# Gate and up weights in 4 MB transfers, and a scatter spread between the last tiles, in a hyena, mLSTM and mixture-of-experts block

## What is computed

```python
def ec_moe(h, w_router, w_gate, w_up, w_down):
    cap = CAP_FACTOR * L // N_EXPERTS                  # 64 tokens for each expert
    aff = jax.nn.softmax((h @ w_router).astype(jnp.float32), axis=-1)
    g, idx = lax.top_k(jnp.swapaxes(aff, 1, 2), cap)
    xs = jax.vmap(lambda hb, ib: hb[ib])(h, idx)
    a = jnp.einsum('becd,edf->becf', xs, w_gate)       # w_gate, w_up: 16 x 1024 x 2048
    u = jnp.einsum('becd,edf->becf', xs, w_up)
    ye = jnp.einsum('becf,efd->becd', jax.nn.silu(a) * u, w_down) * g[..., None]
    # ye's rows are added at their tokens' places; w_down: 16 x 2048 x 1024
```

## Time and profile before

| | |
|---|---|
| median of 3 runs | 1299.17 us (1297.36 to 1302.92) |
| profiled execution | 1296.7 us, its span 1294.7 us |
| TensorE matrix products busy | 1192.9 us, 92% |
| VectorE busy | 342.1 us, 26% |
| ScalarE busy | 164.3 us, 13% |
| GpSimd busy | 33.8 us, 3% |
| moved from memory | 453.02 MB, 352 GB/s over the span |
| DMA issues of gate, up, down tiles to the ring | 63, 63, 61 of 2048 KB, two of 1024 KB |

### The profile page before, as it was taken

One profiled execution on the slowest core, in us unless ns is written; L12 is line 12 of the kernel. 1 busy time (PEld: TensorE's weight loads), 2 busy tenths in 40 slices (PEclk: granted clock), 3 DMA queues, 4 the chain that ended last, 5 costly groups with the idle time before them and its releaser, 6 DMA issues.

```text
span 1294.7 us, 12923 instructions
## 1 busy us (share of the span) xinstructions
PE 1192.9 (92%) x5378; PEld 501.9 (39%) x5378; DVE 342.1 (26%) x625; ACT 164.3 (13%) x350; POOL 33.8 (3%) x61
## 2 busy tenths in 40 slices
PE   5899999999989999999979899998979898888997
PEld 2444454554444353353324253342324234232332
DVE  3775829346450020210201121010201110020140
ACT  2510020034420001000100010000101000000021
POOL 2000020000000001000000000000000000000000
PEclk9999999999999999999999999999999999999999
DMA  9966320306469999999999999999999999999997
GB/s 347 401 227 239 132 82 0 131 1 260 197 247 386 426 429 420 429 428 428 427 428 429 428 427 427 429 428 428 428 429 428 429 428 429 428 428 428 426 427 319
DMA packets 44867, 455.98 MB, mean 352 GB/s; under 512 B 6208, under 2 KB 6320, under 8 KB 16922
## 3 DMA queue, kind: packets, MB, share of 16 engines
q1 hardware_dynamic: 44098, 454.95, 84.2%
q0 software_dynamic: 464, 0.33, 0.1%
q10 hardware_dynamic: 264, 0.11, 0.1%
HBM read 453.02 MB, written 2.36 MB: 352 GB/s over the span
## 4 chain that ended last, share of the span: by engine, by line
PE 64%; DMA 29%; DVE 4%; ACT 1%; issue 1%; SPq 1%; POOL 0%; DVEq 0%; POOLq 0%
DMA ring<-in_w_exp_up 27%; PE B L1259 17%; PE B L1223 14%; PE B L775 6%; PE B L1166 4%; PE B L1022 4%; PE B L903 3%; PE B L1276 3%; PE B L968 2%; DMA ring<-in_pos 2%; PE B L825 2%; PE B L1240 1%; PE B L1176 1%; PE B L1003 1%; PE B L891 1%
## 5 line engine op out<-in xcount | busy, mean ns | idle before, releaser
L1223 PE MATMUL B<-ring,moe 128*64 128x512 f32 x2016 | 448.5, 595 | 64.5 <-DMA ring<-in_w_exp_up 34.8
L1223 PEld LDWEIGHTS B<-ring,moe 128*64 128x64 f32 x2016 | 139.5, 137 | 367.6 <-issue 250.3
L1259 PE MATMUL B<-ring,moe 128*64 128x512 f32 x992 | 217.0, 594 | 0.4 <-issue 0.3
L2219 DVE TENSOR_TENSOR moe<-moe,B 128x512 f32<-128x512 f32 x30 | 19.8, 684 | 611.5 <-PE B L1223 611.5
L1259 PEld LDWEIGHTS B<-ring,moe 128*64 128x64 f32 x992 | 69.8, 137 | 133.3 <-issue 131.1
L775 PE MATMUL B<-ring 128*128 128x512 f32 x192 | 83.6, 594 | 0.0
L1609 ACT ACTIVATE moe<-B 128x512 f32<-128x512 f32 x32 | 17.4, 594 | 385.2 <-PE B L1223 385.2
L1276 PE MATMUL B<-moe 128*128 128x512 f32 x128 | 63.1, 618 | 0.5
L1166 PE MATMUL B<-moe,xl 128*128 128x128 f32 x448 | 56.7, 287 | 1.9 <-DVE moe L2198 1.9
L1166 PEld LDWEIGHTS B<-moe,xl 128*128 128x128 f32 x448 | 55.5, 201 | 2.2 <-DVE moe L2198 2.2
L775 PEld LDWEIGHTS B<-ring 128*128 128x128 f32 x192 | 36.1, 190 | 45.1 <-issue 45.1
(11 more groups left out here) (383 smaller groups left out, 794.8 us busy)
## 6 DMA issues: line engine op xcount, KB each, us to landing
ring<-in_w_exp_up SPq DMA_DIRECT2D x63, 2048.0 KB, 30.0
ring<-in_w_exp_gate SPq DMA_DIRECT2D x63, 2048.0 KB, 28.4
ring<-in_w_exp_down SPq DMA_DIRECT2D x61, 2048.0 KB, 33.9
ring<-in_w_in SPq DMA_DIRECT2D x6, 2048.0 KB, 9.3
ring<-in_w_mod SPq DMA_DIRECT2D x10, 1024.0 KB, 7.5
ring<-in_w_mod SPq DMA_DIRECT2D x4, 2048.0 KB, 14.4
fr<-in_w_mod SPq DMA_DIRECT2D x6, 1024.0 KB, 9.4
ring<-in_w_out SPq DMA_DIRECT2D x2, 2048.0 KB, 7.8
```

Of the source, the lines that this page charges most:

```text
L1223: x = mm(B[2 * up + n // 2][rows, :], xst[:, 2 * q + k, CAP * e2:CAP * (e2 + 1)], w[:, k, n * CH:(n + 1) * CH], start=(q == 0 and k == 0), ...
L1259: x = mm(B[5][CAP * half:CAP * (half + 1), :], hdt[:, q // 2, k * P + at:k * P + at + CAP], wd[:, k, half * CH:(half + 1) * CH], start=(q ...
L2219: v.tensor_tensor(hid[:, m, :], sil[:, m, :], B[2 + m][:, :], ALU.mult).then_inc(S["v_hid"], 1)
```

## The change

Gate and up tiles take four rows to a partition: a block of 512 rows is two tiles, and partition p holds rows 4p to 4p + 3, of which the even tile has the first two and the odd one the last two. `pair_rows` becomes `quad_rows`, every fourth column of a 512-wide stretch, and the vectors, the router's weights and their copies follow. From group 1 on a new function, `expert_pair`, loads two tiles that are neighbours in the ring with one transfer of 4 MiB: for gate and up a piece is 32768 bytes, for down it stays 16384. SP waits for the second tile of a pair to be used and then issues both; TensorE waits only at the first tile of a pair. The tiles of a group go g, g, u, u, g, g, u, u, d, d, d, d, twice; the first expert keeps the old order (`FIRST_TILES`), and group 0 keeps single transfers, with the slots in another order (`SLOT_OF`) and the first loads ordered to suit. In the last expert, g0 g1, u0 u1 and g2 g3 come as pairs, and from tile 6 on (`SINGLE_FROM`) the tiles are single. In `gate_up` of the last expert each of the first four tiles is followed by two scatter products, each of the next three by two of the products that were L1377 (now `last_rows`); the last two and both turns stand behind the last up tile.

```diff
-def pair_rows(k):
-    return slice(2 * P * (k // 2) + k % 2, 2 * P * (k // 2 + 1), 2)
+def quad_rows(k):
+    return slice(4 * P * (k // 4) + k % 4, 4 * P * (k // 4 + 1), 4)
...
-        vr3 = slot(4, 3840, 4096)
+        vr3 = slot(7, 2048, 2560)
...
-        SLOT_OF = [3, 7, 6, 5, 0, 1, 4, 2]
+        SLOT_OF = [6, 7, 4, 5, 0, 1, 2, 3]
...
-            for q in range(4):
-                TILES += [("g", 4 * e2 + q), ("u", 4 * e2 + q)]
+            for q in (0, 2):
+                TILES += [(kind, 4 * e2 + q + n) for kind in "gu" for n in range(2)]
             TILES += [("d", 4 * e2 + q) for q in range(4)]
...
+        FIRST_TILES = [(kind, q) for q in range(4) for kind in "gu"] + TILES[8:]
+        SINGLE_FROM = 6
...
-                    src = w[0, bass.ds(ex, 1), q * 2 * P:(q + 1) * 2 * P, :]
-                    src = src.rearrange("o (p k) n -> p (o k) n", p=P)
+                    src = w[0, bass.ds(ex, 1), (q // 2) * 4 * P:(q // 2 + 1) * 4 * P, :]
+                    src = src.rearrange("o (p k) n -> p (o k) n", p=P)[:, 2 * (q % 2):2 * (q % 2) + 2, :]
...
+            def expert_pair(i, group, after=0):
+                kind, st = TILES[i]
+                e2, q = divmod(st, 4)
+                r = (ring_turn(i, False) - after * HALF) % NSLOT
+                at = SLOT_OF[r] * SLOTF
+                dst = ring[:, at:at + 2 * SLOTF]
+                ex = expert(group, e2, after)
+                if kind == "d":
+                    src = A["w_exp_down"][0, bass.ds(ex, 1), q * CH:(q + 2) * CH, :]
+                    src = src.rearrange("o (b p k) n -> p (o b) (k n)", b=2, p=P)
+                    dst = dst.rearrange("p (b n) -> p b n", b=2)
+                else:
+                    w = A["w_exp_gate" if kind == "g" else "w_exp_up"]
+                    src = w[0, bass.ds(ex, 1), (q // 2) * 4 * P:(q // 2 + 1) * 4 * P, :]
+                    src = src.rearrange("o (p k) n -> p (o k) n", p=P)
+                    dst = dst.rearrange("p (k n) -> p k n", k=4)
+                sp.dma_start(dst, src).then_inc(d_ring[r], 16)
...
             sp.wait_ge(S["p_w"], done_count("i", 5))
+            expert_tile(8, 0)
+            sp.wait_ge(S["p_num"], 16)
             expert_tile(0, 0)
-            sp.wait_ge(S["p_num"], 16)
-            expert_tile(2, 0)
             expert_tile(3, 0)
...
-            expert_tile(7, 0)
+            expert_tile(2, 0)
             sp.wait_ge(S["p_w"], len(DONE))
             expert_tile(4, 0)
             expert_tile(5, 0)
             sp.wait_ge(S["p_lg"], NLT)
             sp.wait_ge(S["p_g1"], 4)
-            expert_tile(8, 0)
+            expert_tile(7, 0)
             expert_tile(23, 0)
...
             with sp.Fori(1, ALONE - 1) as j:
-                for i in range(NTI):
-                    used(i, j)
-                    expert_tile((i + NSLOT) % NTI, j if i + NSLOT < NTI else j + 1)
+                for i in range(0, NTI, 2):
+                    used(i + 1, j)
+                    expert_pair((i + NSLOT) % NTI, j if i + NSLOT < NTI else j + 1)
...
-                    tr(B[0][:, 128:140], vr3[0:12, 0:2 * P:2], upper(12))
-                    tr(B[0][:, 140:152], vr3[0:12, 1:2 * P:2], upper(12)).then_inc(S["p_vt"], 1)
+                    for k in range(4):
+                        x = tr(B[0][:, 128 + 6 * k:134 + 6 * k], vr3[0:6, k:4 * P:4], upper(6))
+                    x.then_inc(S["p_vt"], 1)
...
-                pe.wait_ge(d_ring[r], NTI // NSLOT * 16 * group + 16 * (n + 1))
+                if first or r % 2 == 0:
+                    pe.wait_ge(d_ring[r], NTI // NSLOT * 16 * group + 16 * (n + 1))
...
+                for n, (kind, st) in enumerate(TILES[0:8]):
+                    if n == 0:
                         pe.wait_ge(S["v_xs"], 4 * group + 4)
+                    if n == (0 if last else 4):
                         pe.wait_ge(S["a_xs"], 4 * group + 4)
+                    products(kind, st)
+                    if last and n < NLT:
+                        scatter(group - 1, after, (2 * n, 2 * n + 1))
+                    elif last and n < 2 * NLT - 1:
+                        last_rows(n - NLT)
...
             gate_up(NGROUP - 1, 0, 1, False, True)
-            pe.wait_ge(S["v_yacc"], 8 * (NGROUP - 1))
-            for c in range(NLT):
-                if c == 2:
-                    turn(NGROUP - 1, 0, 1, 0)
-                for half in range(2):
-                    x = mm(B[5][CAP * half:CAP * (half + 1), :], peq[:, c, 0:CAP], y3[:, c, half * CH:(half + 1) * CH],
-                           start=(c == 0), stop=False)
-            x.then_inc(S["p_tail"], 1)
+            last_rows(NLT - 1).then_inc(S["p_tail"], 1)
+            turn(NGROUP - 1, 0, 1, 0)
             turn(NGROUP - 1, 0, 1, 1)
```

More of the change, by code:

```diff
@@ L438, in expert_tile @@
             def expert_tile(i, group, after=0, last=False):
-                kind, st = TILES[i]
+                first = isinstance(group, int) and group == 0
+                kind, st = (FIRST_TILES if first else TILES)[i]
                 e2, q = divmod(st, 4)
-                first = isinstance(group, int) and group == 0
                 r = (ring_turn(i, first) - after * HALF) % NSLOT
@@ L516, in _ @@
                     expert_tile(in_ring[n + NSLOT], 0)
-                else:
-                    expert_tile(n + NSLOT - len(in_ring), 1)
-            with sp.Fori(1, ALONE - 1) as j:
-                for i in range(NTI):
-                    used(i, j)
-                    expert_tile((i + NSLOT) % NTI, j if i + NSLOT < NTI else j + 1)
[L523 to L527, removed]
-                    expert_tile(HALF + i + NSLOT - NTI, ALONE, 1)
@@ new lines, in _ @@
+            for i in range(0, NTI, 2):
+                used(i + 1, ALONE - 1)
+                if i + NSLOT < NTI:
+                    expert_pair(i + NSLOT, ALONE - 1)
+                else:
+                    expert_pair(HALF + i + NSLOT - NTI, ALONE, 1)
+            for i in range(HALF, NTI, 2):
+                used(i + 1, ALONE, 1)
+                expert_pair((i + NSLOT) % NTI, ALONE if i + NSLOT < NTI else ALONE + 1, 1)
+            with sp.Fori(ALONE + 1, NGROUP - 2) as j:
+                for i in range(0, NTI, 2):
+                    used(i + 1, j, 1)
+                    expert_pair((i + NSLOT) % NTI, j if i + NSLOT < NTI else j + 1, 1)
@@ L536, in _ @@
+            for i in range(0, NTI, 2):
+                t = i + NSLOT - NTI
+                if t < SINGLE_FROM:
+                    used(i + 1, NGROUP - 2, 1)
+                    expert_pair((i + NSLOT) % NTI, NGROUP - 2 if t < 0 else NGROUP - 1, 1)
+                    continue
+                for n in range(2):
+                    used(i + n, NGROUP - 2, 1)
+                    expert_tile(t + n, NGROUP - 1, 1)
             for i in range(HALF - NSLOT):
@@ L1198, in gate_up, with products @@
             def gate_up(group, e2, after, first=False, last=False):
-                for q in range(4):
-                    wg = ring_tile("g", 4 * e2 + q, group, after, first).rearrange("p (k n) -> p k n", k=2)
-                    if first and e2 == 0:
+                def products(kind, q):
+                    up = kind == "u"
+                    w = ring_tile(kind, 4 * e2 + q, group, after, first).rearrange("p (k n) -> p k n", k=2)
+                    for k in range(2):
+                        for n in range(4):
+                            rows = slice(CAP, P) if n % 2 else slice(0, CAP)
+                            x = mm(B[2 * up + n // 2][rows, :], xst[:, 2 * q + k, CAP * e2:CAP * (e2 + 1)],
+                                   w[:, k, n * CH:(n + 1) * CH],
+                                   start=(q == 0 and k == 0), stop=(q == 3 and k == 1))
+                    x.then_inc(S["p_gu"], 1)
+                if first and e2 == 0:
+                    for q in range(4):
                         if q == 0:
```

70 lines of the change are left out of this document (31 added, 39 removed).

## The result

The changed kernel takes **1319.34 us** (median of 4 runs, 1319.05 to 1322.39) against 1298.74 for the kernel before beside it: a ratio of **1.0158, 95% interval 1.0131 to 1.0186**, 20.6 us slower. The forecast was 1297.6 us. The profiled execution has a span of 1317.1 us, 22.4 more than before.

A forecast was written before the change was run, and what follows sets the result against it. The prediction took the weight stream, unbroken since 391 us, to bound the kernel. Terms of -4.0, -0.7, +2.6 and +0.5 summed to -1.6 us, giving 1297.6 us, range 1292.5 to 1303.0.

The forecast's parts named there:

- Bound: Whole kernel: the weight stream, unbroken since 391 us, sets the end; only the last 30 us are TensorE's own.
- Start: Group 0's new slots, load order and step-four reads, priced from transpose weight loads (208 against 209 ns), cost nothing.
- Later issue: Pairs issued when both tiles are used: the queue runs nearly dry at group 1's first tile, 2.6 us lost.
- Rival D: The queue runs dry at more places, near 484 and 533 us, 1 to 1.5 us each: 1300; chance 0.06.
- Larger pieces: Gate and up pairs: 440 fewer pieces per engine at 9.0 ns each, 4.0 us gained.
- rival A: 32768-byte pieces move no faster per byte or are cut in two; both gains go: 1302.3; chance 0.18.
- C: Rival: larger pieces are slower in the pairs, at 410 GB/s 23.7 us plus 3.1: 1326; chance 0.09.
- Fewer transfers: 81 pairs replace 162 transfers, so each engine posts 81 completions less, at 9 ns each: 0.7 us gained.
- The last expert: TensorE waits for pair g2, g3, then works 32.8 us to the down product's end: 0.5 us lost.
- a sign of being wrong: Tail: the way from the g2, g3 pair's landing to the end more than 1 us off 40.6 us.
- Sum: All terms, -4.0 - 0.7 + 2.6 + 0.5 = -1.6 us, making 1297.6 us on the median of 1299.17.
- the second term: Later issue of pairs at the first tile of group 1: 2.6 us lost.

The follow-up runs named there:

- e1: The kernel before with the four-row layout alone, single 2 MB transfers, old tile order and old tail: 1311.34 us, ratio 1.0106.
- e12: e10 with GpSimd regrouping the last quarter of `x3` only at 429 us, so the first gathers read it with a step: 1299.77 us, ratio 1.0009.
- e2: The changed kernel with the two-row layout, so pairs of 4 MB with pieces of 16384 bytes: 1303.10 us, ratio 1.0045.
- e9: e2 with single tiles in group 1 and for the last two experts, 16384-byte pieces: 1299.59 us, ratio 1.0010.
- e3: The changed kernel with `x3` regrouped by VectorE during group 0, so that later gathers read it without a step: 1307.12 us, ratio 1.0072.
- e5: The changed kernel with x regrouped by GpSimd before the first gather, so that no gather has a step: 1303.2 us, ratio 1.0030.
- e6: e5 with single tiles in group 1 and in the whole last expert: 1300.19 us, ratio 1.0006.
- e7: e2 with single transfers for all twelve tiles of the last expert: 1304.19 us, ratio 1.0032.
- e10: e9 with the four-row layout, 32768-byte pieces in the pairs and GpSimd's regrouping from e5: 1299.31 us, ratio 1.0007.

## Why the prediction was wrong, step by step

**Bound.** Right. The stream sets the time until the last 60 us (30 in the forecast), and lost bytes account for the loss.

**Start: wrong, and the step that failed.** "Rows read with a step of four instead of two ... So nothing" took its price from the earlier trace rows. Those rows are weight loads of transposes, and what is loaded there is the identity, without any step; the strided data is the moving operand. The gathers load the strided data as weights. The right row for the price did not exist in the trace of before, and the rule that the prediction used elsewhere, to bound a missing price from both sides, was not applied here. e1 measured it: 134 ns a load, 3.7 us for a half gather of 32, and 14.5 us of stream, since TensorE is the slower of the two up to 515 us and every strided load of group 0 and of the entry to group 1 counts, 64 in each. Some of it is a later first gather (388.31 us in e1, 388.88 in the changed kernel), whose cause is open like that of e12. Behind 515 us e1 loses nothing more.

**Later issue.** Right in mechanism and place, and right in size where nothing else is changed: 2.5 us at 487 to 515 us in e2, forecast 2.6. Group 0's part of the stream lost 1.2 us more (409 for 414 GB/s), 0.8 of them by a first gather at 387.89 instead of 387.08 us. In the changed kernel the same wait met longer gathers: together 10.7 us, and at 780 to 800 us, which the forecast called safe because the shortest way there was 17.1 us, another 5.9. The 17.1 us were a slack in a schedule with gathers of 3.8 us. Rival D named the mechanism (the queue dry at more places), near 484 and 533 us and for 1 to 1.5 us each. e9 shows such a place at 770 us even with a step of two, worth 1.1 us.

**Larger pieces.** Right: -4.0 us forecast, and the two undisturbed windows of the changed kernel give -1.2 - 2.8 = -4.0. The windows round to whole GB/s, half of one is 0.8 us there, and they cover only part of the pairs, so the agreement to a tenth is luck; the size is not. The windows of e3, e5 and e6 from 600 to 1200 us show the 430 GB/s that the forecast asked for, and e2's is 428, so it is the pieces and not the transfers. Packets fell from 44867 to 36274, by 8593. Of these, 1546 are of under 512 bytes (6208 and 4662 on the pages); the other 7047 are the forecast's 7040. No piece is cut, so rival A is out, and so is C. The Trainium skill (DMA: Bandwidth & Descriptors, Why small descriptors are slow), with the 3.5 ns a piece that the prediction estimated from it, would have made it 1.6 us, some 429 GB/s; the windows side with the 9.0 ns of the rows.

**Fewer transfers.** -0.7 forecast. e2, which has the transfers but not the pieces, keeps 428. The 0.7 us would be 0.4 GB/s, less than a window resolves, so the term is neither confirmed nor refuted.

**The last expert.** 0.5 us forecast, 3.0 measured: from the landing of the last expert's second tile (u0 before, g1 after) to the end of the down product it was 1235.03 to 1286.90 us before, 51.9, and is 1254.42 to 1309.34, 54.9. The forecast let TensorE wait for the pair g2, g3. In the chain it does not wait for it:

```profile
1225.59 28.83 DMA ring<-in_w_exp_gate
1254.42 0.14 issue
1254.56 3.65 PE B L1243 x16
1258.21 1.91 PE B L1322 x4
...
1289.65 3.43 PE B L1243 x16
1293.08 0.86 PE B L1277 x4
1293.94 1.40 PE B L1286 x8
1295.33 0.03 issue
1295.37 13.98 PE B L1305 x64
```

Its last wait is for g0, g1, and from 1254.56 us there are eight tiles with four scatter pairs between them, 1.91 us each, which the forecast left out of TensorE's own sum because the stream had covered them. With the pairs, they are no longer covered. The pair g2, g3, issued at 1247.00 us, lands 27.7 us later, at 1274.7, when TensorE has just done the fourth of the eight tiles; it comes to g2 at 1276.62, so it does not wait for the pair. From the landing to the end of the span that is 42.4 us, not 40.6, which the forecast had named as a sign of being wrong. So was a stream that starts later than 391 us: the transfer that went out at 390.51 us before goes out at 393.75. e7 and e9 show that the delay begins one expert earlier.

**Sum.** Stretches of the stream 6.2 + 10.7 - 1.2 + 5.9 - 2.8, last expert 3.0: 21.8 of the span's 22.4 us. Of them the forecast had the -4.0, 2.6 us of the second term, and 0.5 of the last. By cause, e1 gives 13.1 us at the end, e2 4.8, and what is left of the 20.6 is 2.7, near the 1.9 us of the hole at 780 us less the gain of the pieces.

## What to carry to other kernels

A layout that gives a DMA longer pieces is paid for by whoever reads the tile with a step, and on TensorE the operand decides: ask for every strided read whether it is loaded as weights or moves, and take the price from a row of the same side. Where two changes each draw on the same slack (here the depth of a queue during a stretch in which nothing is used up), check the sum against the slack, not each alone. Joining transfers moves the issue to the later and the wait to the slower of two tiles; keep single tiles wherever the queue is short and for so long before the end that the consumer can still catch up, here two experts.

## What the runs showed of the hardware

- The stationary load of 128x128 float32 costs 192, 196, 329 and 335 ns (medians) at a step of 1, 2, 4 and 8 elements. With the strided data as the moving operand, a product of the transposes takes 283 ns at a step of two and 284 at four.
- Pieces of 32768 bytes in two thirds of the stream's bytes: 430 instead of 428 GB/s.
- A VectorE product took 1.03 us instead of 0.22 while GpSimd copied beside it, and ended 0.08 us after the copy (e10 against e12).
- The granted clock of TensorE over 600 to 1200 us was 1.00 before and 0.97 in e3, e9, e10 and e12, in which TensorE waits up to 3.5 to 5.0 us at a time for a pair (2.5 before); a mean between the two levels, 1.2 and 2.4 GHz. Behind a wait of 2.80 us at 608 us in e9 two tiles took 8.79 us instead of 7.09, at a granted clock of 0.89 over 610 to 620 us. TensorE was busy for 547.01 us of the 600 in e9 and 536.30 before. The stream moved 427 to 430 GB/s there in all of them, so no time at the end is shown to hang on it.
